# Last state products of a head moved ahead of the branch product's last quarter, projection quads loaded earlier, gate and branch fetched in four parts

## The chip, the core and the metric

One core of a Trainium2 chip. It has five engines with a queue of instructions each: TensorE (PE in the profile; its weight loads are shown apart as PEld), VectorE (DVE), ScalarE (ACT), GpSimd (POOL) and SyncE (SP), which here only issues transfers. Engines meet through semaphores alone. Matmul results land in PSUM, in eight banks that go round. The metric is the time of one execution on the device, in microseconds (us); lower is better.

## The reference, cut to what matters

One layer of a streaming encoder for 512 new frames and 8 x 16 next frames, 640 rows in all, in fp32:

```python
x = LN1(ALPHA*x + 0.5*swiglu(x, ffn1))
cb, cc, ch, q, k, v, g, gc, gr = split(x @ w_in)
y_conv = (cb * causal_conv3(cc * ch)) @ w_conv_br
o, S_new = retention(rotary(q), rotary(k), v, S)     # 4 heads, dk 256, dv 512
#   S_new = gamma^L * S + k_decayed^T @ v            # one state for each of 8 streams and each head
y_ret = (group_norm(o) * silu(g)) @ w_ret_br
h = (sigmoid(gc)*y_conv + sigmoid(gr)*y_ret) @ w_out
x = LN2(ALPHA*x + h);  x = LN3(ALPHA*x + 0.5*swiglu(x, ffn2))
```

The states `S_new` of the 8 streams and 4 heads are outputs as well (2 x 256 x 512 fp32 for each pair of streams and head slot, 512 KB a transfer).

## The kernel before

Every fp32 product is made of three matmuls of split operands: `xh, xl` are the high and low parts of `x`, `wh, wl` of the weights. ScalarE or VectorE makes the parts of activations; a chunk of weights (128 x 1024) is fetched twice, as `raw` by SP and as `wh` by GpSimd's queue, and GpSimd subtracts them into `wl` (L525). Three chunk buffers go round; a chunk's buffer is released (`chunk_used`) by the first matmul after its last use. TensorE's next chunk needs `chunk_split`, GpSimd's word that `wl` is there.

Stages in order: the first FFN (groups of "quads", a form of Strassen product over 4 weight blocks that SP loads into `qraw` two ahead, and "natural" down products), the layer norm LN1 with transposes, the projections (two units of gates by `first_units`, two more units, then 25 quads with spills to memory, then the conv branch), four retention heads (`head(i)`), the output projection (`natural` with `merged_ready` waits), LN2, the second FFN, LN3.

PSUM: every product takes the next place in a running count `bk`; the bank is the place modulo 8. `bank()` (TensorE) waits until `psum_free` says that the place eight earlier has been read. VectorE raises `psum_free` strictly in its own order of instructions, so a bank is free only when VectorE has come to it. A head has 72 places (`HEAD_BANKS`); names `U_...` are places within it. `SKIPPED` is a number of places passed over to make the sum come out.

The end of a head on TensorE: the branch product `og @ w_ret` in four chunks `m` = 0 to 3, each of two units (unit 2m and 2m+1, 24 matmuls of 128x320 each, two places a unit), and the state products `vp, km` (a matmul of 128x512 for each half of a state). Group 1 of the states has its last two slots after `m = 0`; group 0 has all four slots, eight matmuls, after `m = 3`. VectorE takes what they make: `branch(u)` adds unit u to the sum `yr` (`z<-ps,z` in the profile; `yr` lies in `z`), `new_state` adds two products to each slot's state (`state<-state,ht,ps`, L1801), `rotate_query(i + 1)` turns the next head's query (six instructions that write `rope` and `rot`), and stands after `branch(4)`. ScalarE: `masked_keys` makes `km`, `state_store` sends finished states out, then `state_load(i, 0)` waits until they have landed and loads group 0 anew, and `table_load` fetches the next head's table `ht`.

In the last head, `merge(u)` multiplies the finished sum by the gate `gate_r` and adds the other branch `mix`; ScalarE's `merge_hi` copies it to `xh`, and VectorE's `merge_lo(u)` makes `xl`; the output projection waits for both. `gate_r` and `mix` (8 x 640 columns each) are fetched by SP in two parts (units 0-1, units 2-7) when the last head comes to place `U_T`, and SP's weight loads stand behind them. On ScalarE `merge_hi(range(6))` stands behind `state_load(i, 0)`. When all merges are done ScalarE loads `z` (2560 KB) for LN2.

At the start of the projections VectorE frees the eight places of the four gate units by one memset (`banks_freed(8)`, L1538), after the low parts of the first quad and two sums for the second.

## Time and profile before

| | |
|---|---|
| median of 3 runs | 1887.28 us (1886.36 to 1888.89) |
| the profiled execution | 1886.21 us |
| its span in the trace | 1884.4 us |
| granted TensorE clock, mean | 0.984 of full speed |
| TensorE busy | 1805.5 us, 96% of the span |
| VectorE, ScalarE, GpSimd busy | 1267.0, 614.3, 577.8 us |

The span runs from the first to the last instruction of the program. The profiled execution's time is 1.8 us more than its span. TensorE is busy nearly all the time, so a reader looks for the few places where it is not: a row of its timeline ends in brackets with the idle time before it and the engine that ended it. Most of the idle time beside the places told below is at the layer norms and at both ends of the span, which the change does not touch. A stretch's granted clock (1.00 is 2.4 GHz, 0.50 is 1.2 GHz) stands in the rows by windows.

### The profile page before, as it was taken

To read this page: it belongs to the slowest core of one execution; us is meant where nothing else is said; L and a number is where in the kernel's file an instruction comes from. 1 tells how busy PE (TensorE), PEld (TensorE's weight loads), DVE (VectorE), ACT (ScalarE), POOL (GpSimd) and SP (SyncE) were. 2 spreads that over 40 slices of the span, in tenths; PEclk is the share of its full clock that TensorE was granted. 3 is DMA by queue.
4 is the path that set the end of the run, shared out by engine and by line. 5 is a ranking of instruction groups with operands and counts; after the bars stand their busy time and mean duration, and the time that the engine had idled before them with its cause. 6 is when DMAs were issued, how large, how long until landed. Compare 5 with 4: busy or idle time off the path is not lost. (4 is left out here: it accounts for less than half of the span.)

```text
span 1884.4 us, 26852 instructions
## 1 busy us (share of the span) xinstructions
PE 1805.5 (96%) x10900; PEld 1676.7 (89%) x10900; DVE 1267.0 (67%) x1635; ACT 614.3 (33%) x1038; POOL 577.8 (31%) x378
## 2 busy tenths in 40 slices
PE   7999999997899999999999999999797999999996
PEld 6989899896899999999898898988777889899895
DVE  7768486577787778743667565665838767585666
ACT  4325233241444444410421405133104224243240
POOL 5324232232242222114323232331234323233230
PEclk9999999998999999999999999999898999999998
DMA  8332423304543334258457484765754333324312
GB/s 296 127 128 79 135 86 117 134 23 157 179 134 118 118 109 130 70 183 299 156 199 251 157 310 162 240 228 215 269 198 150 123 103 104 129 71 131 123 45 101
DMA packets 88314, 286.80 MB, mean 152 GB/s; under 512 B 8704, under 2 KB 11136, under 8 KB 87680
## 3 DMA queue, kind: packets, MB, share of 16 engines
q1 hardware_dynamic: 40832, 151.80, 24.9%
q10 hardware_dynamic: 29792, 69.32, 9.9%
q0 software_dynamic: 17568, 63.97, 9.8%
q8 instruction: 87, 1.43, 0.3%
q14 instruction: 35, 0.29, 0.0%
HBM read 247.76 MB, written 37.30 MB: 151 GB/s over the span
## 5 line engine op out<-in xcount | busy, mean ns | idle before, releaser
L525 POOL TENSOR_TENSOR wl<-raw,wh 128x1024 fp32r<-128x1024 f32 x122 | 319.3, 2619 | 100.1 <-DMA wh<-in_weights 88.6
L602 PE MATMUL ps<-th,wql 128*128 128x320 f32 x1040 | 321.3, 309 | 0.5 <-ACT pu L996 0.5
L602 PE MATMUL ps<-th,wqh 128*128 128x320 f32 x1040 | 321.1, 309 | 0.0
L602 PE MATMUL ps<-tl,wqh 128*128 128x320 f32 x1040 | 320.6, 308 | 0.0
L516 POOL DMA_DIRECT2D wh<-in_weights x122 | 68.3, 560 | 691.9 <-PE ps L602 630.9
L1354 DVE TENSOR_TENSOR wql<-qraw,wqh 128x512 fp32r<-128x512 f32 x195 | 242.4, 1243 | 24.9 <-ACT wqh L996 24.9
L996 ACT ACTIVATE pu<-ps 128x320 f32<-128x320 f32 x195 | 85.4, 438 | 506.8 <-PE ps L602 506.8
L602 PE MATMUL ps<-xh,wql 128*128 128x320 f32 x780 | 240.6, 308 | 3.3 <-DVE mv L1538 1.9
L602 PE MATMUL ps<-xl,wqh 128*128 128x320 f32 x780 | 240.5, 308 | 0.0
L602 PE MATMUL ps<-xh,wqh 128*128 128x320 f32 x780 | 240.5, 308 | 0.0
L1354 DVE TENSOR_TENSOR wql<-quad_s,wqh 128x512 fp32r<-128x512 f32 (+1 forms) x195 | 180.5, 925 | 55.5 <-ACT wqh L996 55.1
L539 POOL TENSOR_TENSOR quad_s<-qraw 128x512 f32<-128x512 f32 x65 | 84.3, 1298 | 394.1 <-DVE wql L1354 394.1
L1598 DVE SCALAR_TENSOR_TENSOR z<-ps,z 128x512 f32<-128x512 f32 x130 | 87.9, 690 | 166.6 <-PE ps L602 166.1
L602 PEld LDWEIGHTS ps<-th,wql 128*128 128x128 f32 x1040 | 195.3, 188 | 1.2 <-ACT pu L996 0.8
L602 PEld LDWEIGHTS ps<-tl,wqh 128*128 128x128 f32 x1040 | 195.3, 188 | 0.5
L602 PEld LDWEIGHTS ps<-th,wqh 128*128 128x128 f32 x1040 | 195.3, 188 | 0.0
L602 PE MATMUL ps<-wh,hl 128*128 128x512 f32 x440 | 175.3, 398 | 7.0 <-DVE hl L1354 3.4
L602 PE MATMUL ps<-xh,wl 128*128 128x320 f32 x480 | 154.1, 321 | 25.0 <-POOL wl L525 13.6
L602 PE MATMUL ps<-wh,hh 128*128 128x512 f32 x440 | 174.3, 396 | 0.0
L602 PE MATMUL ps<-wl,hh 128*128 128x512 f32 x440 | 174.2, 396 | 0.0
L996 ACT ACTIVATE wqh<-quad_s 128x512 fp32r<-128x512 f32 (+1 forms) x195 | 149.9, 769 | 48.4 <-PE ps L602 46.8
L602 PE MATMUL ps<-xl,wh 128*128 128x320 f32 x480 | 152.4, 318 | 0.0
(180 smaller groups left out, 3753.9 us busy)
## 6 DMA issues: line engine op xcount, KB each, us to landing
qraw<-in_quads SPq DMA_DIRECT2D x130, 512.0 KB, 3.6
raw<-in_weights SPq DMA_DIRECT2D x122, 512.0 KB, 3.8
wh<-in_weights POOLq DMA_DIRECT2D x122, 512.0 KB, 5.0
state<-in_state_ret ACTq DMA_DIRECT2D x48, 512.0 KB, 7.5
out_ret_sample<-state ACTq DMA_DIRECT2D x32, 512.0 KB, 5.1
qk_scratch<-ctp SPq DMA_DIRECT2D x8, 640.0 KB, 5.5
z_scratch<-z ACTq DMA_DIRECT2D x1, 2560.0 KB, 7.5
z<-gate_c_scratch SPq DMA_DIRECT2D x4, 640.0 KB, 6.4
```

What stands on the lines that cost most here:

```text
L516: pool.dma_start(wh[:, c % NSPL, :], a["weights"][c]).then_inc(hi_loaded[c % NSPL], 16)
L525: pool.tensor_tensor(wl[:, r, :], raw[:, r, :], wh[:, r, :].bitcast(f32), ALU.subtract).then_inc(chunk_split, 1)
L539: pool.tensor_tensor(qs[:, 0, :], qraw[:, c0, 512:1024], qraw[:, c1, 512:1024], ALU.add).then_inc(pool_sums, 1)
L602: ins = nc.tensor.matmul(out, lhs, rhs, start=start, stop=stop, skip_group_check=adds)
L996: return nc.scalar.activation(out, in_, ACT.Copy, **kw)
L1354: return V.tensor_tensor(out, x, y, op)
L1598: V.scalar_tensor_tensor(out=zt, in0=ps[:, b, :], scalar=scale, in1=zt, op0=ALU.mult, op1=ALU.add).then_inc(psum_free, 1)
```

## The change

Four edits. (1) TensorE makes the eight products of group 0 before chunk `m = 3`, at places 56 to 63, and units 6 and 7 come after them at places 64 to 67; four places are passed over. VectorE accordingly takes `new_state` before `branch(6)` and `branch(7)`, and in the last head its merges stand in another order. ScalarE issues the next head's table at the end of the head, without waiting for all banks. (2) SP loads the first two quads of the projections within the last group of the first FFN, before that FFN's last weight chunk. (3) VectorE frees the eight places in two halves, the first after three low parts. (4) `gate_r` and `mix` are fetched in four parts of two units, with one weight chunk after the first and one after the third part; ScalarE copies three high parts before the last states are sent out and five after.

```diff
 # SP
-                if n == QUAD_START[stage] + QUAD_COUNT[stage]:
+                if n == QUAD_START[stage] + QUAD_COUNT[stage] + (NQRAW if stage == 0 else 0):
                     return
...
             def projections():
-                load_quad(1)
-                load_quad(1)
                 load(6)
...
-            for n, ms in enumerate((slice(0, 2), slice(2, KT))):
+            for n in range(KT // 2):
+                ms = slice(2 * n, 2 * n + 2)
                 sync.dma_start(gate_r[:, ms, :], a["gate_r"][:, ms, :]).then_inc(gate_r_in[n], 16)
                 sync.dma_start(mix[:, ms, :], a["mix"][:, ms, :]).then_inc(mix_in[n], 16)
-            load(2 + KT)
+                if n in (0, 2):
+                    load(1)
+            load(KT)
 # PE
-        U_O1, U_S1A, U_G3, U_T, U_SP, U_OUT, U_S1B, U_S0 = 25, 26, 30, 32, 38, 40, 44, 64
+        U_O1, U_S1A, U_G3, U_T, U_SP, U_OUT, U_S1B, U_S0 = 25, 26, 30, 32, 38, 40, 44, 56
                 for m in range(4):
+                    if m == 3:
+                        assert bk.at - u0 == U_S0
+                        state_products(0, range(4))
...
                 bk.add(SKIPPED)
-                state_products(0, range(4))
 # ACT
                 if i:
-                    act.wait_ge(psum_free, bk())
-                    table_load(i)
...
                 if i == H - 1:
-                    merge_hi(range(6))
+                    merge_hi(range(3))
                 state_store(i, 0, range(4), u0 + U_S0)
+                if i < H - 1:
+                    table_load(i + 1)
 # DVE, projections
-                for what in (A11, S12, A12, S3, A22, S4):
+                for what in (A11, S12, A12):
+                    quad_lo_part(n, what)
+                dve.wait_ge(gate_made, 2)
+                banks_freed(4)
+                for what in (S3, A22, S4):
                     quad_lo_part(n, what)
...
-                banks_freed(8)
+                banks_freed(4)
 # DVE, head
                 if i < H - 1:
-                    for m in range(2, KT):
-                        branch(m, SKIPPED if m == KT - 1 else 0)
+                    for m in range(2, 6):
+                        branch(m)
                         if m == 4:
                             rotate_query(i + 1)
                     new_state(range(4), 3)
+                    branch(6)
+                    branch(7, SKIPPED)
                     return
```

In heads 0 to 2, on VectorE, from the last updates of group 1 to the first of the next head. Before:

```order
L1354 TENSOR_TENSOR z<-ps,z 128x640 [waits psum_full] x3
L1354 TENSOR_TENSOR rope<-q_raw,cos 128x640 [waits dve_step,qk_in]
L1354 TENSOR_TENSOR rope<-q_raw,sin 128x640
L1354 TENSOR_TENSOR rot<-q_raw,sin 128x640
L1354 TENSOR_TENSOR rot<-q_raw,cos 128x640
L1354 TENSOR_TENSOR rot<-rope,rot 128x640 [waits dve_step]
L1354 TENSOR_TENSOR rot<-rope,rot 128x640
L1354 TENSOR_TENSOR z<-ps,z 128x640 [waits psum_full,dve_step]
L1354 TENSOR_TENSOR z<-ps,z 128x640 [waits psum_full] x2
L1801 SCALAR_TENSOR_TENSOR state<-state,ht,ps 128x512 [waits psum_full,state_in0]
```

And in the changed kernel:

```order
L1358 TENSOR_TENSOR z<-ps,z 128x640 [waits psum_full] x3
L1358 TENSOR_TENSOR rope<-q_raw,cos 128x640 [waits dve_step,qk_in]
L1358 TENSOR_TENSOR rope<-q_raw,sin 128x640
L1358 TENSOR_TENSOR rot<-q_raw,sin 128x640
L1358 TENSOR_TENSOR rot<-q_raw,cos 128x640
L1358 TENSOR_TENSOR rot<-rope,rot 128x640 [waits dve_step]
L1358 TENSOR_TENSOR rot<-rope,rot 128x640
L1358 TENSOR_TENSOR z<-ps,z 128x640 [waits psum_full,dve_step]
L1809 SCALAR_TENSOR_TENSOR state<-state,ht,ps 128x512 [waits psum_full,state_in0]
```

The three `z<-ps,z` are `branch(2)` to `branch(4)`, the one after the rotation is `branch(5)`; `branch(6)` and `branch(7)` moved behind the eight updates, the rotation kept its place.

In the last head, on VectorE, from `branch(2)` on. Before:

```order
L1354 TENSOR_TENSOR z<-ps,z 128x640 [waits psum_full]
L1354 TENSOR_TENSOR z<-z,gate_r 128x640 [waits psum_free,mix_in0,gate_r_in0]
L1354 TENSOR_TENSOR z<-z,mix 128x640 [waits dve_step]
L1354 TENSOR_TENSOR z<-ps,z 128x640 [waits psum_full]
L1354 TENSOR_TENSOR z<-z,gate_r 128x640 [waits psum_free]
L1354 TENSOR_TENSOR z<-z,mix 128x640 [waits dve_step]
L1354 TENSOR_TENSOR xl<-z,xh 128x640 [waits merged_hi]
L1354 TENSOR_TENSOR z<-ps,z 128x640 [waits psum_full]
```

And in the changed kernel:

```order
L1358 TENSOR_TENSOR z<-ps,z 128x640 [waits psum_full]
L1358 TENSOR_TENSOR xl<-z,xh 128x640 [waits merged_hi]
L1358 TENSOR_TENSOR z<-z,gate_r 128x640 [waits psum_free]
L1358 TENSOR_TENSOR z<-z,mix 128x640 [waits dve_step]
L1358 TENSOR_TENSOR z<-ps,z 128x640 [waits psum_full]
L1358 TENSOR_TENSOR xl<-z,xh 128x640 [waits merged_hi]
L1358 TENSOR_TENSOR z<-ps,z 128x640 [waits psum_full]
L1358 TENSOR_TENSOR z<-z,gate_r 128x640 [waits psum_free,mix_in1,gate_r_in1]
L1358 TENSOR_TENSOR z<-z,mix 128x640 [waits dve_step]
L1809 SCALAR_TENSOR_TENSOR state<-state,ht,ps 128x512 [waits psum_full,state_in0]
```

Here the first row is `branch(3)` (`branch(2)` and `merge(0)` before it stayed), then `merge_lo(0)`, `merge(1)`, `branch(4)`, `merge_lo(1)`, `branch(5)`, `merge(2)`, and the state updates; before, five merges and `branch(7)` stood ahead of those updates.

On SP, around the end of the first FFN:

```order
+L418 DMA qraw<-in_quads 128x1024 [waits quad_ready] x6
+L407 DMA raw<-in_weights 128x1024 [waits chunk_used] x7
 L418 DMA qraw<-in_quads 128x1024 [waits quad_ready] x2
 L407 DMA raw<-in_weights 128x1024 [waits chunk_used]
-L418 DMA qraw<-in_quads 128x1024 [waits quad_ready] x4
-L407 DMA raw<-in_weights 128x1024 [waits chunk_used] x6
```

Four of the quad loads that stood between the FFN's last chunk and the next six stand before that chunk now.

## Rows read from the trace of the kernel before

**Rows 1.** The page, busy time of each engine, share of the span, instructions.

```profile
PE 1805.5 (96%) x10900; PEld 1676.7 (89%) x10900; DVE 1267.0 (67%) x1635; ACT 614.3 (33%) x1038; POOL 577.8 (31%) x378
```

**Rows 2.** TensorE's waits: engine, line <- for whom: us in total, times, longest.

```profile
PE ps L602 <- POOL wl L525: 21.6, 6, 11.0
```

**Rows 3.** Timeline of TensorE, end of head 2: start, us, instruction, [idle before <-releaser].

```profile
1218.35 0.31 PE L602 MATMUL ps<-ogh,wl 128*128 128x320 f32 x1
...
1225.39 0.62 PE L602 MATMUL ps<-vp,km 128*128 128x512 f32 x2
...
1226.63 1.63 PE L602 MATMUL ps<-vp,km 128*128 128x512 f32 x6 [0.62 <-DVE z L1354]
1228.10 0.39 PE L602 MATMUL ps<-wh,xl 128*128 128x512 f32 x1
```

**Rows 4.** Timeline of VectorE, same place.

```profile
1219.64 3.02 DVE L1354 TENSOR_TENSOR rot<-rope,rot 128x640 f32<-128x640 f32 x1
1222.76 0.82 DVE L1354 TENSOR_TENSOR z<-ps,z 128x640 f32<-128x640 f32 x1
...
1226.40 5.34 DVE L1801 SCALAR_TENSOR_TENSOR state<-state,ht,ps 128x512 f32<-128x512 f32 x8
```

**Rows 5.** Timeline of GpSimd, same place.

```profile
1219.55 2.44 POOL L525 TENSOR_TENSOR wl<-raw,wh 128x1024 fp32r<-128x1024 f32 x1
```

**Rows 6.** Line L1160, the four state loads issued from 1212.2 to 1213.9.

```profile
DMA to landing us min/median/max: 5.6/7.0/9.1
```

**Rows 7.** By windows: stretch, length, busy (xstarted) of PE, PEld, DVE, ACT, POOL, PEclk, DMA.

```profile
439.60:443.00 3.40, 3.40 (x10) 2.63 (x9) 1.39 (x2) 0.00 (x0) 1.51 (x2) 0.50 0.00 0
1330.50:1333.90 3.40, 3.40 (x15) 3.40 (x14) 0.15 (x1) 0.49 (x1) 2.38 (x1) 0.50 1.04 313
1334.00:1337.40 3.40, 3.40 (x25) 3.40 (x24) 3.19 (x5) 0.81 (x3) 0.00 (x0) 1.00 0.92 296
504.50:507.90 3.40, 3.18 (x22) 3.21 (x23) 0.15 (x3) 0.96 (x2) 0.00 (x0) 1.00 0.66 152
```

**Rows 8.** Timelines of TensorE, SP and GpSimd at the first FFN's end.

```profile
438.69 0.50 PE L602 MATMUL ps<-wh,hl 128*128 128x512 f32 x1 [3.08 <-POOL wl L525]
...
427.87 2.49 SPq L418 DMA_DIRECT2D qraw<-in_quads  x4
...
427.76 0.57 POOL L516 DMA_DIRECT2D wh<-in_weights  x1 [25.02 <-PE ps L602]
...
436.30 2.33 POOL L525 TENSOR_TENSOR wl<-raw,wh 128x1024 fp32r<-128x1024 f32 x1 [7.97 <-DMA wh<-in_weights]
```

**Rows 9.** The page, issues: engine, count, KB each, median us from issue to landing.

```profile
wh<-in_weights POOLq DMA_DIRECT2D x122, 512.0 KB, 5.0
```

**Rows 10.** Timeline of TensorE, first quad of the projections.

```profile
504.72 0.38 PE L602 MATMUL ps<-xh,wql 128*128 128x320 f32 x1 [1.85 <-DVE mv L1538]
```

**Rows 11.** Timeline of TensorE, last head and output projection.

```profile
1329.16 0.41 PE L602 MATMUL ps<-ogh,wl 128*128 128x320 f32 x1 [2.81 <-POOL wl L525]
...
1352.42 1.19 PE L602 MATMUL ps<-vp,km 128*128 128x512 f32 x2 [6.92 <-DVE z L1354]
...
1355.12 0.63 PE L602 MATMUL ps<-wh,xl 128*128 128x512 f32 x1
...
1379.03 0.50 PE L602 MATMUL ps<-wh,xl 128*128 128x512 f32 x1 [2.04 <-POOL wl L525]
```

**Rows 12.** Timelines of ScalarE and VectorE in the last head.

```profile
1331.17 2.19 ACTq L1160 DMA_DIRECT2D state<-in_state_ret  x4
...
1334.17 0.82 DVE L1354 TENSOR_TENSOR xl<-z,xh 128x640 fp32r<-128x640 f32 x1 [3.52 <-ACT xh L996]
...
1338.85 3.29 DVE L1354 TENSOR_TENSOR z<-z,gate_r 128x640 f32<-128x640 f32 x1
```

**Rows 13.** Line L1310, the load of z issued at 1363.35.

```profile
DMA to landing us min/median/max: 12.5/12.5/12.5
```

**Rows 14.** Timeline of GpSimd in the last head.

```profile
1339.05 2.41 POOL L525 TENSOR_TENSOR wl<-raw,wh 128x1024 fp32r<-128x1024 f32 x1
```

More of the change, by code:

```diff
@@ L325, in build_layer @@
         qk_in = sem("qk_in")
-        gate_r_in, mix_in = ([sem(f"{name}{i}") for i in range(2)] for name in ("gate_r_in", "mix_in"))
+        gate_r_in, mix_in = ([sem(f"{name}{i}") for i in range(KT // 2)] for name in ("gate_r_in", "mix_in"))
         merged_sum, merged_hi, merged_ready = sem("merged_sum"), sem("merged_hi"), sem("merged_ready")
@@ L392, in build_layer @@
         U_V, U_SC, U_G, U_O0, U_OP, U_G2 = 0, 10, 14, 18, 19, 23
-        U_O1, U_S1A, U_G3, U_T, U_SP, U_OUT, U_S1B, U_S0 = 25, 26, 30, 32, 38, 40, 44, 64
-        SKIPPED = U_S0 - U_S1B - 4 - (2 * KT - 4)
-        assert U_S0 + 8 == HEAD_BANKS
+        U_O1, U_S1A, U_G3, U_T, U_SP, U_OUT, U_S1B, U_S0 = 25, 26, 30, 32, 38, 40, 44, 56
+        SKIPPED = HEAD_BANKS - U_S0 - 8 - 4
+        assert U_S0 == U_S1B + 4 + 8
         @block.sync
@@ L956, in head @@
                 bk.add(SKIPPED)
-                state_products(0, range(4))
+                assert bk.at - u0 == HEAD_BANKS
             def projections():
@@ L1305, in _ @@
                 head(i)
-            merge_hi(range(6, KT))
+            merge_hi(range(3, KT))
             act.wait_ge(psum_free, bk())
@@ L1841, in merge @@
                 def merge(m):
-                    if m in (0, 2):
+                    if m % 2 == 0:
                         dve.wait_ge(gate_r_in[m // 2], 16)
@@ L1868, in head @@
                 merge(0)
-                for m in range(1, 5):
-                    branch(m + 2)
+                branch(3)
+                merge_lo(0)
+                merge(1)
+                branch(4)
+                merge_lo(1)
+                branch(5)
+                merge(2)
+                new_state(range(4), 3)
+                merge_lo(2)
+                branch(6)
+                merge(3)
+                branch(7, SKIPPED)
+                for m in range(4, KT):
                     merge(m)
                     merge_lo(m - 1)
-                merge(5)
-                merge_lo(4)
-                branch(KT - 1, SKIPPED)
-                new_state(range(4), 3)
-                merge_lo(5)
-                merge(6)
-                merge(7)
-                merge_lo(6)
-                merge_lo(7)
+                merge_lo(KT - 1)
             for i in range(H):
```

## The prediction, made before the changed kernel ran

> **What bounds the kernel now.** I read the page first: TensorE is busy 96% of the span [rows 1], so a change can only pay or cost through TensorE's idle stretches and through what they do to its clock. The list of TensorE's waits comes next: waiting for GpSimd's low parts of the weights is the longest entry, 21.6 us in six times [rows 2]. Then I went through TensorE's timeline from gap to gap, and beside each gap read the engine that ended it. The reader is to see three places that the change touches: the end of each head [rows 3 to 6], the end of the first FFN with the start of the projections [rows 8 to 10], and the last head with the start of the output projection [rows 11 to 14]. Everything between them is TensorE without gaps, which merely shifts.
>
> The clock is the second thing to see. In the 3.4 us from 1330.5 the granted clock is 0.50 (1.2 GHz) and TensorE starts 15 matmuls; in the 3.4 us from 1334.0 it is 1.00 (2.4 GHz) and it starts 25 of the same kind [rows 7]. One such low stretch costs about ten matmuls of 0.147 us, 1.5 us. One followed the idle 2.81 us before 1329.16, and one (from 439.6) the idle 3.08 us before 438.69; none followed the idle 1.85 us before 504.72 [rows 7, 8, 10, 11].
>
> **Part 1, heads 0 to 2: the state products before the last quarter.** Before, the last quarter (units 6 and 7) runs from 1218.35 to 1225.39, then come eight products, of which the third waits 0.62 us, and the next head's matmuls start at 1228.10 [rows 3]. After, the eight products stand at 1218.35. What matters is which PSUM bank each takes. Eight banks go round; the products take places 56 to 63 of the head, so the one in place 62 needs place 54 free, a bank of unit 5. `branch(5)` frees it on VectorE, and the changed code has `rotate_query` between `branch(4)` and `branch(5)`, as before. Before, nobody was waiting for `branch(5)`: unit 7 took places 58 and 59 and needed only places 50 and 51. The rotation's last addition takes 3.02 us, and `branch(5)` starts at 1222.76 [rows 4].
>
> So, on the old time axis: six products from 1218.35 at 0.24 us (six took 1.47 us before the next head [rows 3]) end at 1219.8. `branch(5)` is through at 1223.5, 0.74 after its start; TensorE resumed 0.23 us after such a point (1226.63 against 1226.40 [rows 3, 4]), so the seventh product starts at 1223.73: 3.9 us idle. Unit 6 takes places 64 and 65 and needs the first two products added to the state: two updates of 0.67 us (eight took 5.34 [rows 4]) after 1223.5, plus 0.23, is 1225.06; a second wait of 0.8 us. Then 7.04 us for units 6 and 7 brings the next head to 1232.10 against 1228.10: **+4.0 us per head**, the vanished 0.62 included. Units 6 and 7 now run while VectorE ends its updates, and `branch(7)` follows at once, so the next head finds its banks. Three heads: +12.0. An idle stretch of 3.9 us, with a second behind it, lies beyond the 2.81 us that already cost a low stretch of clock, so I add one each: +1.5 x 3 = 4.5, bounds 0 and three low stretches each (13.5), of which the row nearest in length shows one. **Together +16.5, bounds +12 and +25.5.** The four loads that the state updates wait for are early enough: those of head 2 were issued by 1213.9 and landed 9.1 us later at the latest [rows 6], by 1223, and the last is wanted at 1227.5.
>
> The table load that ScalarE now issues at the head's end, without its wait, removes a wait of VectorE of a few microseconds; VectorE is ahead of TensorE there, so its price is nothing.
>
> **Part 2, the quads loaded earlier.** At 427.5 SP issues the last weight chunk of the first FFN and behind it, within 2.5 us, four quad loads; GpSimd's half of the same chunk is issued at 427.76, its low part can only start at 436.30, and TensorE stands 3.08 us until 438.69 [rows 8]. In the changed order the four loads are issued during the last two quads, some 20 us earlier, into buffers that nobody needs. A transfer of GpSimd's takes 5.0 us in the median [rows 9], which gives 432.8, the low part (2.33 us) at 435.2: just in time for TensorE, which would go on at 435.4. That is -3.0 (bounds -3.1 and -2.0 if it lands a microsecond later), and the low stretch from 439.6 goes too, -1.5. The chain behind it (layer norm, transposes) hangs on these matmuls and moves with them. The cover that could fail is small: a GpSimd instruction lengthening one of the norm's on VectorE, 2 us either way.
>
> **Part 3, the banks freed by halves.** TensorE waits 1.85 us until 504.72 for a memset that stands behind six of VectorE's instructions [rows 10]. The first quad needs three banks of the first two units, and these are freed before those six now; the other four banks are wanted some 7 us later. -1.85, no bounds worth naming. **Parts 2 and 3: -6.4, bounds -3 and -8.5.**
>
> **Part 4, the last head: loads in four parts, merges in another order.** The weight chunk behind two small and two large loads comes late: TensorE idles 2.81 us until 1329.16. It idles 6.92 us more until 1352.42, where the third state product waits for `branch(7)` behind the merges, and the output projection starts at 1355.12 at the low clock, since its first matmul takes 0.63 us against 0.39 in head 2 [rows 3, 11]. After, the chunk stands behind two small loads alone, so TensorE reaches the state products at 1326.2 + 7.0 = 1333.2. But VectorE is not there. `merge_lo(0)` needs ScalarE's high part, and ScalarE is held until the state stores have landed; it issues the state loads at 1331.17, for 2.19 us, and VectorE gets its first high part at 1334.17 [rows 12]. The bytes in flight are the same, so I keep this. From 1334.17 VectorE now has before the first bank for unit 6: `merge_lo(0)`, `merge(1)`, `branch(4)`, `merge_lo(1)`, `branch(5)`, `merge(2)` (eight instructions of 0.74 to 0.85 us each, 6.2 us), one collision with GpSimd of 2.4 us (such an instruction takes 3.29 instead of 0.82 [rows 12]), and two updates of 0.67: 1344.1. Unit 6 starts at 1344.2; with 7.04 us and 2 us for the clock the projection starts at 1353.2, against 1355.12: -1.9. The low clock within the projection, which I take to last some 2.7 us there, is over by then, -1.2. The wait of 2.04 us until 1379.03 [rows 11] comes of the 2560 KB load of `z` (12.5 us to landing [rows 13]) beside a weight chunk; that load moves with the last merge, and so may hit the next chunk: half of it, -1.0. **Part 4: -4.1.** Bounds: all of it (TensorE from 1333.2 without a wait, 13 + 1.2 + 2.0) is -16.2; if the state stores land 3 us later and each piece behind slips, +3.
>
> **Sum**: 16.5 - 6.4 - 4.1 = +6.0. The profiled execution took 1886.21 us, 1.07 less than the median of the runs, 1887.28; 1886.2 + 6.0 = 1892.2, and by the median 1893.3.
>
> **Rivals.**
> (a) *The rotation's last addition is not lengthened*; this is the one that ends faster. GpSimd's instruction starts at 1219.55 and VectorE's at 1219.64, 0.09 us apart [rows 4, 5]. The chunk is now released by a product of 128x512 (0.39 us) in place of a matmul of 128x320 (0.31 us), about 0.08 us later, so the two may change places. If VectorE then keeps its 0.82 us, each head loses 4.0 - 2.2 = 1.8 us, and idle stretches under 2 us leave the clock: 5.4 - 6.4 - 4.1 = -5.1, 1882.2. It decides at that 0.09 us. Against it: at 1338.85 VectorE started 0.20 us before GpSimd (1339.05) and still took 3.29 us [rows 12, 14]. [...]
> (b) *The last head pays in full*: the merges do not hold TensorE; -16.2 in place of -4.1: 16.5 - 6.4 - 16.2 = -6.1, 1881.2. For it: two waits and two low stretches stand there. Against it: ScalarE's state stores.
> (c) *Stalls without the clock, last head a little better*: +12.0 - 6.4 - 6 = -0.4, 1886.9.
> (d) *The clock stays low over the end of each head* (three low stretches, as after the 6.92 us): 25.5 - 6.4 - 4.1 = +15.0, 1902.3; with the last head at its bad bound 1909.
> (e) The change does not do what it says: TensorE finds the banks free. Code and order exclude it.
>
> **How the numbers follow.** Forecast 0.48, 1893.3 with its own range 1890 to 1898. (d) 0.14. (c) 0.25. (a) 0.06 and (b) 0.07. A measurement of this kernel tells about 0.2%, 3.8 us, from no change: slower than 1891.1 holds (d) and most of the forecast, 0.61; within 0.2% holds (c) and a rest of the forecast, 0.26; faster holds (a) and (b), 0.13. The range 1884 to 1904 leaves (a), (b) and the end of (d) out.
>
> **What would show it.** In heads 0 to 2: a gap of about 3.9 us between the sixth and the seventh state product, ended by VectorE, a second of 0.8 before unit 6, and a clock of 0.50 for 3.4 us thereafter. No gap near 435 and 500. In the last head no wait for GpSimd in the branch, but some 9 us between the first state product and unit 6. I am wrong if VectorE's `branch(5)` starts within 2 us of unit 5's end, or if the state loads of the last head are issued well before 1328.

## The result, and the profile after

The changed kernel takes **1893.93 us** in the median of eight runs (1893.04 to 1900.13), the kernel before 1888.43 us in runs beside it: a ratio of 1.0039 (95%: 1.0029 to 1.0049). It is slower: by 5.5 us in the medians, by 5.5 to 9.3 us by the ratio, beyond the 0.2% that a measurement tells. Its profiled execution took 1893.32 us, with a span of 1891.5 us against 1884.4.

The page shows hardly anything of this. Engine busy times (share of the span, instructions), to be held against [rows 1]:

```profile
PE 1808.1 (96%) x10900; PEld 1678.7 (89%) x10900; DVE 1272.2 (67%) x1636; ACT 614.5 (32%) x1038; POOL 579.8 (31%) x378
```

The matmuls are the same 10900. Their busy time grew by 2.6 us and the span by 7.1, so idle time and slower matmuls both took part. The list of TensorE's waits (line, for whom: us in total, times, longest) says more:

```profile
PE ps L603 <- POOL wl L526: 16.2, 3, 11.0
PE ps L603 <- DVE z L1358: 13.8, 4, 5.7
PE ps L603 <- DVE z L1844: 3.8, 1, 3.8
PE ps L603 <- DVE state L1809: 2.7, 3, 1.7
```

GpSimd's entry fell from 21.6 us in six waits to 16.2 in three [rows 2]. Below it stand VectorE's `z` (the branch products' results, by which a bank comes free) and `state` (the state updates, which free the banks of the state products).

**End of head 2.** TensorE's timeline (start, us, instruction, [idle before <-releaser]), the answer to [rows 3]:

```profile
1223.35 1.55 PE L603 MATMUL ps<-vp,km 128*128 128x512 f32 x6
1228.75 0.95 PE L603 MATMUL ps<-vp,km 128*128 128x512 f32 x2 [3.84 <-DVE z L1358]
1230.06 0.61 PE L603 MATMUL ps<-ogh,wl 128*128 128x320 f32 x1 [0.36 <-DVE state L1809]
```

Six of eight state products run, then TensorE stands for 3.84 us. In heads 0 and 1 it is 3.84 us as well (until 986.99 and 1108.23). VectorE's timeline there, the answer to [rows 4], and GpSimd's:

```profile
1224.64 3.04 DVE L1358 TENSOR_TENSOR rot<-rope,rot 128x640 f32<-128x640 f32 x1
1227.78 0.82 DVE L1358 TENSOR_TENSOR z<-ps,z 128x640 f32<-128x640 f32 x1
```

```profile
1224.64 2.35 POOL L526 TENSOR_TENSOR wl<-raw,wh 128x1024 fp32r<-128x1024 f32 x1
```

The addition that ends the rotation takes 3.04 us beside GpSimd's instruction; `branch(5)` stands behind it at 1227.78, and the seventh product starts at 1228.75, 0.23 us after VectorE has gone on to its next instruction (1228.52).

**The clock.** Windows (stretch, length, busy (xstarted) of PE, PEld, DVE, ACT, POOL; granted clock; DMA share; GB/s) behind the gap of head 0:

```profile
986.70:990.10 3.40, 2.99 (x9) 2.33 (x10) 3.40 (x7) 0.00 (x0) 0.00 (x0) 0.50 0.35 129
990.10:993.50 3.40, 3.40 (x14) 3.40 (x14) 2.01 (x4) 0.00 (x0) 0.00 (x0) 0.50 1.00 375
993.50:996.90 3.40, 3.40 (x25) 3.40 (x25) 0.83 (x1) 0.00 (x0) 0.00 (x0) 1.00 0.76 255
```

Two stretches at the lower level (0.50, 1.2 GHz) follow this gap, with 14 matmuls in the full one where 25 run at 2.4 GHz. Heads 1 and 2 have one such stretch each (1109.5 to 1113.0, 1229.0 to 1232.4).

**End of the first FFN and first quad.** GpSimd, then TensorE, the answers to [rows 8] and [rows 10]:

```profile
432.33 2.41 POOL L526 TENSOR_TENSOR wl<-raw,wh 128x1024 fp32r<-128x1024 f32 x1 [4.66 <-DMA wh<-in_weights]
```

```profile
497.10 0.31 PE L603 MATMUL ps<-xh,wql 128*128 128x320 f32 x1
```

GpSimd's half of the last chunk now lands in time, and neither gap is left.

**Last head.** VectorE, ScalarE and TensorE, the answers to [rows 11] and [rows 12]:

```profile
1344.59 3.07 DVE L1358 TENSOR_TENSOR xl<-z,xh 128x640 fp32r<-128x640 f32 x1 [7.20 <-ACT xh L1000]
```

```profile
1341.72 2.06 ACTq L1164 DMA_DIRECT2D state<-in_state_ret  x4
```

```profile
1350.14 1.19 PE L603 MATMUL ps<-vp,km 128*128 128x512 f32 x2 [5.71 <-DVE z L1358]
1351.76 1.19 PE L603 MATMUL ps<-vp,km 128*128 128x512 f32 x2 [0.44 <-DVE z L1358]
1354.67 0.60 PE L603 MATMUL ps<-ogh,wl 128*128 128x320 f32 x1 [1.72 <-DVE state L1809]
...
1363.62 0.40 PE L603 MATMUL ps<-wh,xl 128*128 128x512 f32 x1
...
1394.78 0.50 PE L603 MATMUL ps<-wh,xl 128*128 128x512 f32 x1 [1.74 <-DVE z L1606]
```

VectorE sits idle for 7.20 us, since ScalarE holds the high part back until the stores have landed and it has issued four state loads. TensorE then waits for VectorE three times. The output projection starts at full clock now (first matmul 0.40 us, 0.63 before), and the wait inside it is one for the load of `z`.

**By stages**, from landmarks in TensorE's timeline (us from one to the next):

| stage | before | after | difference | predicted |
|---|---|---|---|---|
| first FFN's first quad to first transpose of the norm | 392.15 | 387.30 | -4.85 | -4.5 |
| that transpose to the projections' first quad | 51.82 | 49.64 | -2.18 | -1.85 |
| head 0 | 114.88 | 121.95 | +7.07 | +5.5 |
| head 1 | 114.86 | 120.44 | +5.58 | +5.5 |
| head 2 | 114.87 | 120.05 | +5.18 | +5.5 |
| last head | 127.02 | 125.37 | -1.65 | -1.9 |
| output projection | 58.07 | 56.49 | -1.58 | -2.2 |

The seven sum to +7.6; the stages between are within 0.6 us of before, and the span grew by 7.1. These are single traces. The sections on experiment 4 and on part 4 tell how far the first, the second and the last row vary between traces of the same code.

### The profile page after: what moved, and what is told of

The parts are those of the page before. It is cut to its first block and busy times, and to the rows that moved or that the text cites. A ratio compares the mean times of both kernels' runs of the same rounds, so it can differ in the third digit from the quotient of the medians.

```text
span 1891.5 us, 26860 instructions
## 1 busy us (share of the span) xinstructions
PE 1808.1 (96%) x10900; PEld 1678.7 (89%) x10900; DVE 1272.2 (67%) x1636; ACT 614.5 (32%) x1038; POOL 579.8 (31%) x378
## 5 line engine op out<-in xcount | busy, mean ns | idle before, releaser
L603 PE MATMUL ps<-xh,wl 128*128 128x320 f32 x480 | 153.7, 320 | 27.6 <-POOL wl L526 16.2
L1000 ACT ACTIVATE wqh<-quad_s 128x512 fp32r<-128x512 f32 (+1 forms) x195 | 149.9, 769 | 48.4 <-PE ps L603 46.7
```

The costliest lines, as they stand in the source:

```text
L603: ins = nc.tensor.matmul(out, lhs, rhs, start=start, stop=stop, skip_group_check=adds)
L1000: return nc.scalar.activation(out, in_, ACT.Copy, **kw)
```

## The experiments

Each ratio is to executions of the kernel before that ran beside the experiment's own; `last_sum_behind` alone has a single execution and no ratio. "Gap" is an idle stretch of TensorE.

**1. The rotation in two parts** (`split_rotation`): in the changed kernel the products of the rotation move to behind `branch(2)`, and only its two sums stay behind `branch(4)` (`rotate_products` and `rotate_sums` are the rotation's first four and last two instructions; their definitions are left out here).

```diff
                     for m in range(2, 6):
                         branch(m)
+                        if m == 2:
+                            dve.wait_ge(qk_in, 32 * (i + 2))
+                            rotate_products(q_raw)
                         if m == 4:
-                            rotate_query(i + 1)
+                            rotate_sums()
```

> The changed kernel, with the rotation of the next head's query split on VectorE: its four products stand behind branch(2), its difference and sum behind branch(4), in place of all six behind branch(4). Nothing is left out. Theory (TensorE waits for branch(5) because the rotation stands ahead of it): VectorE waits 2.7 us before branch(3), so four products of 0.74 us fit there, and the last two end before unit 5 does; the gap of 3.84 us before the seventh state product goes in heads 0 to 2, 0.3 to 0.8 us before unit 6 stay (two state updates), and the low clock behind it goes. By landmarks each head gets 4.1 us plus 1.5 us (3.0 in the first) shorter: 17 to 18 us in all, 1876 us against 1893.9, and about 12 us faster than the kernel before. Rival (the place of the state products costs by itself, by banks or by late state loads): a gap of 2 us or more stays before unit 6 and the time is 1886 or more.

Measured: **1878.29 us**, ratio 0.9944 (0.9932 to 0.9956). TensorE before unit 6 of head 2:

```profile
1213.81 0.85 PE L603 MATMUL ps<-vp,km 128*128 128x512 f32 x3
1215.24 0.39 PE L603 MATMUL ps<-ogh,wl 128*128 128x320 f32 x1 [0.58 <-DVE state L1815]
```

VectorE there:

```profile
1209.40 0.82 DVE L1358 TENSOR_TENSOR z<-ps,z 128x640 f32<-128x640 f32 x1 [2.54 <-PE ps L603]
1210.14 1.55 DVE L1358 TENSOR_TENSOR rot<-rope,rot 128x640 f32<-128x640 f32 x2
1212.95 0.82 DVE L1358 TENSOR_TENSOR z<-ps,z 128x640 f32<-128x640 f32 x1 [1.25 <-PE ps L603]
```

The last row is `branch(5)`: VectorE now waits for TensorE before it, not the other way round. The gap of 3.84 us is gone, no low stretch of the clock is left in the three heads, and each takes 114.8 us where the changed kernel takes 120.05 to 121.95. So the six instructions of the rotation behind `branch(4)` are the cause of the whole loss in the heads. The edit does two things at once: the four products are out of `branch(5)`'s way, and the two sums (1.55 us for both) run before GpSimd's instruction, so that the last of them takes 0.8 us in place of 3.04. How the 3.84 us divide between the two was not measured; if the lengthening is worth its 2.2 us (3.04 less 0.82), an estimate, the order has the other 1.6.

The three heads are 18.0 us shorter, as expected, yet the median fell by 15.6 us, to 1878.29 and not to 1876. The traces account for most of the difference: the first FFN's first quad starts 1.9 us later here (62.06 against 60.16 us; 60.08 to 62.72 in the thirteen traces), and the last head is 0.6 us longer.

And 114.8 is what a head took before: put before the last quarter, the state products gain nothing, since the 0.62 us ahead of their third [rows 3] comes back as 0.58 ahead of unit 6.

**2. Is it the split alone?** (`before_split_rotation`): the same edit in the kernel before.

> The kernel before with the rotation split as in split_rotation. Nothing is left out. Theory (nobody waits for branch(5) in the old order): no difference, within 0.5 us of the kernel before; the gap of 0.62 us before the third state product stays. If it gains 2 us or more, part of what split_rotation gained has nothing to do with the change.

Measured: **1887.55 us**, ratio 1.0002 (0.9993 to 1.0012), no difference, as expected; the 0.62 us ahead of the third product stays. VectorE's queue at the head's end only matters once somebody waits in it.

**3. Only the last sum behind `branch(5)`** (`last_sum_behind`, one run): five of the rotation's six instructions stay ahead (the parameter `last`, which leaves the sixth out, is not shown).

```diff
-                            rotate_query(i + 1)
+                            rotate_query(i + 1, last=False)
+                    step(tt(rot[:, 1, :], rope[:, 1, :], rot[:, 1, :], ALU.add))
                     new_state(range(4), 3)
```

> The changed kernel, with one instruction moved: the last addition of the rotation (the one that takes 3.04 us beside GpSimd's) stands behind branch(5) in place of ahead of it, in heads 0 to 2. Nothing is left out. Theory: the seventh state product starts 3.0 us earlier (gap 0.8 in place of 3.84), but the updates of the state stand behind the addition now, so the gap before unit 6 grows from 0.4 to 0.6 by the same 3 us, and each head is as long as in the changed kernel within 0.5 us: 1891.5 us of span. If a gap of some 3.8 us stays before the seventh product, branch(5) is not what it waits for.

Measured: 1893.26 us. VectorE, then TensorE:

```profile
1224.69 0.82 DVE L1358 TENSOR_TENSOR z<-ps,z 128x640 f32<-128x640 f32 x1
1225.43 2.32 DVE L1358 TENSOR_TENSOR rot<-rope,rot 128x640 f32<-128x640 f32 x1
```

```profile
1225.66 0.71 PE L603 MATMUL ps<-vp,km 128*128 128x512 f32 x2 [0.71 <-DVE z L1358]
```

```profile
1229.21 0.61 PE L603 MATMUL ps<-ogh,wl 128*128 128x320 f32 x1 [2.85 <-DVE state L1811]
```

`branch(5)` comes early and the gap before the seventh product falls to 0.71 us, but the long addition now stands ahead of the state updates, for which unit 6 waits 2.85 us. Each head takes 119.5 us, heads 1 and 2 that is 0.6 to 1.0 us less than in the changed kernel. The wait was moved, not removed. The three heads together take 4.0 us less than in the changed kernel, and still the time is the same: in this trace the first FFN's first quad starts 2.6 us later, and 0.9 us are lost between the transposes and the projections. With one execution, no more can be read from the time.

**4. The projections' edits alone** (`projections_alone`, `quads_alone`, `banks_alone`): each made in the kernel before, together and apart.

```diff
-                if n == QUAD_START[stage] + QUAD_COUNT[stage]:
+                if n == QUAD_START[stage] + QUAD_COUNT[stage] + (NQRAW if stage == 0 else 0):
...
-                load_quad(1)
-                load_quad(1)
                 load(6)
```

That is `quads_alone`; `banks_alone` has the hunk with `banks_freed(4)` in place of `banks_freed(8)`.

> The kernel before with two of the four parts alone: the first two quads of the projections loaded before the first FFN's last weight chunk, and the banks of the gate units freed in two halves. Nothing is left out. Theory: the gap of 3.08 us near 438 goes with the low clock behind it (4.6 to 4.9 us), the gap of 1.85 us near 504 goes (1.9 to 2.2), and nothing else changes: 6.4 to 7.0 us under the kernel before, 1881.5. Rival (time won ahead of the heads is given back in the conv branch or the heads, which transfers bound): under 4 us faster.

> The kernel before with the quad loads of the projections moved forward and nothing else. Part 2 of the prediction priced this at -4.5 us: the gap of 3.08 us ahead of 438.69 and the low clock behind it go, and the gap of 1.85 us ahead of 504.72 (a memset behind six instructions of VectorE) stays. Both edits together gave -8.4 us between the first quad of the first FFN and the first quad of the projections. If the terms are separate, this kernel has about -6 us there and 1882 to 1883 us in all. Rival: the two gaps have one cause, the late start of what follows the FFN, so that this edit alone takes both: -8.4 us and 1880 to 1881 us, and no gap ahead of the projections' first quad.

> The kernel before with the banks freed by halves and nothing else. Part 3 priced it at -1.85 us: the gap ahead of the projections' first quad goes, the gap of 3.08 us at the end of the first FFN stays: about 1886.3 us. Rival (the two gaps have one cause): the gap ahead of the first quad is only there because of the work that is queued on VectorE, and stays or comes back two quads later: no gain.

| kernel | median, us | ratio (95%) | FFN's first quad to transpose | transpose to first quad |
|---|---|---|---|---|
| before | 1888.43 | | 392.15 | 51.82 |
| `quads_alone` | 1883.59 | 0.9978 (0.9969 to 0.9988) | 387.64 | 51.00 |
| `banks_alone` | 1886.46 | 0.9991 (0.9981 to 1.0002) | 391.12 | 49.47 |
| `projections_alone` | 1880.93 | 0.9966 (0.9954 to 0.9978) | 387.14 | 48.40 |

TensorE at the two places in `quads_alone`:

```profile
435.72 0.50 PE L600 MATMUL ps<-wh,hl 128*128 128x512 f32 x1 [0.22 <-POOL wl L523]
...
499.37 0.38 PE L600 MATMUL ps<-xh,wql 128*128 128x320 f32 x1 [1.85 <-DVE mv L1536]
```

and in `banks_alone`:

```profile
438.65 0.73 PE L602 MATMUL ps<-wh,hl 128*128 128x512 f32 x1 [2.15 <-POOL wl L525]
...
502.33 0.31 PE L602 MATMUL ps<-xh,wql 128*128 128x320 f32 x1
```

The terms are separate, against the rival of one common cause: each edit removes its own gap and leaves the other. Against the trace of before, the early loads give 4.5 us up to the transposes, as priced, and the freed banks 2.35 us behind them against 1.85. But the stage varies where its code is the same: without the early loads it took 392.15, 391.12 (`banks_alone`) and 389.94 us (`before_split_rotation`, whose gap of 2.50 us was followed by no low clock), with them 387.1 to 387.6 in ten traces. So the loads are worth 2.3 to 5.0 us, and the 4.5 us of the forecast need the low stretch. The stage behind the transposes took 51.0 to 52.0 us without the freed banks and 48.4 to 50.5 with them. Of the whole time the ratios make it -4.2 us for the loads, -6.4 us for both, and -1.7 us for the banks, an interval that reaches across no change: shown for the stage, not for the kernel. My expectation of 1882 to 1883 us for `quads_alone` was too low by 0.6 to 1.6 us; the 1886.3 for `banks_alone` and the 1881.5 for `projections_alone` held within 0.6.

**5. The last head: high parts first** (`high_first`): in the changed kernel, ScalarE makes the first two high parts before it waits for the state stores.

```diff
+                if i == H - 1:
+                    merge_hi(range(2))
                 for slot in range(4):
                     act.wait_ge(state_out[slot], i * 32 + 16)
                 state_load(i, 0)
                 if i == H - 1:
-                    merge_hi(range(3))
+                    merge_hi(range(2, 3))
```

> The changed kernel, with ScalarE making the high parts of merged units 0 and 1 before it waits for the state stores of the last head, and only unit 2 behind the state loads. Nothing is left out. Theory (in the last head VectorE stands 7.2 us for ScalarE's first high part, which is held by the landing of the stores): that wait falls under 1 us, merge(1), branch(4) and branch(5) are done by 1344, TensorE waits under 1 us for the first six state products, and unit 6 then waits for the state load alone (landed 1345.99 in the changed kernel): it starts at 1347.5 to 1348.5 on that kernel's axis in place of 1354.67. 6 to 8 us faster than the changed kernel, 1886 to 1888. Rival (the merges themselves are too much work for VectorE there, or the state load bounds): under 2 us are gained.

Measured: **1891.25 us**, ratio 1.0015 (1.0006 to 1.0023), by the medians 2.7 us below the changed kernel where I expected 6 to 8. A miss. ScalarE, then VectorE and TensorE:

```profile
1345.56 2.41 ACTq L1164 DMA_DIRECT2D state<-in_state_ret  x4
```

```profile
1351.52 1.41 DVE L1811 SCALAR_TENSOR_TENSOR state<-state,ht,ps 128x512 f32<-128x512 f32 x2 [1.72 <-DMA state<-in_state_ret]
```

```profile
1344.60 2.08 PE L603 MATMUL ps<-vp,km 128*128 128x512 f32 x8
...
1353.07 0.61 PE L603 MATMUL ps<-ogh,wl 128*128 128x320 f32 x1 [6.39 <-DVE state L1811]
```

VectorE's idle 7.20 us are gone and all eight products run without a wait, so ScalarE's order was one link. But the second state store landed 12.1 us after its issue (both took 9.5 in the changed kernel), the loads went out at 1345.56, and unit 6 waits 6.39 us for the updates. A second chain, store, load, update, lay close behind the first. The last head fell from 125.4 to 122.3 us.

**6. Both** (`split_and_high`): experiments 1 and 5 together.

> Both edits together. If they touch separate places, as the theory has it, the gains add: 17.5 + 7 us, 1869 to 1870 us. If the one only moves a wait that the other pays, it stays above 1873.

Measured: **1873.96 us**, ratio 0.9922 (0.9909 to 0.9935), above the 1869 to 1870 expected, with a gap of 4.58 us before unit 6 from the same chain. I had set 1873 as the mark above which one edit only moves a wait that the other pays, but that mark counted on 7 us from experiment 5, which brought 2.7. With the gains as measured they add, within what the medians tell: 1878.29 less 2.7 is 1875.6.

**7. A load for each slot** (`loads_by_slot`): as 6, but each state load goes out when its own store has landed, and VectorE's state updates come before `merge(2)`.

```diff
                 for slot in range(4):
+                    if slot == 2 and i == H - 1:
+                        merge_hi(range(2))
                     act.wait_ge(state_out[slot], i * 32 + 16)
-                state_load(i, 0)
+                    act.dma_start(state[:, slot, :].rearrange("p (k e) -> p k e", k=2),
+                                  dram_state("state_ret", 0, slot, i)).then_inc(state_in[slot], 16)
...
+                new_state(range(4), 3)
                 merge(2)
-                new_state(range(4), 3)
                 merge_lo(2)
```

> The kernel with both edits (rotation split, two high parts first), with two more: ScalarE issues each slot's state load as soon as that slot's own store has landed, in place of all four after the last store; and in the last head VectorE takes the eight state updates before merge(2). Nothing is left out. In high_first the chain behind unit 6 was: store of slot 3 landed 1345.46, loads issued 1345.56, slot 0 landed 1351.50, first update 1351.52, unit 6 at 1353.07. Theory (unit 6 now waits for a load that is held by other slots' stores): slot 0's load is issued some 10 us earlier and is there in time, the gap before unit 6 (4.58 us in split_and_high) falls to 1 us or less and no low clock follows: 5 to 6 us less, 1868 to 1869. Rival (the transfers there are bound by their sum, an earlier load only makes the store or the weights later): under 1.5 us less than 1873.96.

Measured: **1870.46 us**, ratio 0.9907 (0.9894 to 0.9921): it beats both kernels. ScalarE, VectorE, TensorE:

```profile
1315.15 1.03 ACTq L1301 DMA_DIRECT2D state<-in_state_ret  x2
```

```profile
1328.45 2.75 DVE L1818 SCALAR_TENSOR_TENSOR state<-state,ht,ps 128x512 f32<-128x512 f32 x4 [1.24 <-DMA state<-in_state_ret]
1333.61 2.82 DVE L1818 SCALAR_TENSOR_TENSOR state<-state,ht,ps 128x512 f32<-128x512 f32 x4 [2.40 <-DMA state<-in_state_ret]
```

```profile
1330.00 0.39 PE L603 MATMUL ps<-ogh,wl 128*128 128x320 f32 x1 [1.93 <-DVE state L1818]
...
1340.52 0.47 PE L603 MATMUL ps<-wh,xl 128*128 128x512 f32 x1 [3.23 <-DVE z L1361]
...
1370.17 0.50 PE L603 MATMUL ps<-wh,xl 128*128 128x512 f32 x1 [1.28 <-POOL wl L526]
```

Against experiment 6 the median is 3.5 us lower, but the two intervals overlap. The gap before unit 6 falls to 1.93 us where I expected 1 us or less, no low clock follows it, and the last head takes 119.7 us (121.5 in experiment 6). The first two loads are issued 94.3 us into the head, not 103.5 as in the changed kernel, but VectorE waits for them until 1328.45, 13.3 us after the issue. The updates of the later slots wait 2.40 us more, and the `branch(6)` behind them is late for the output projection.

**8. `branch(6)` and `branch(7)` ahead of the merges** (`branches_first`), as 7 otherwise:

```diff
                 new_state(range(4), 3)
+                branch(6)
                 merge(2)
+                branch(7, SKIPPED)
                 merge_lo(2)
-                branch(6)
                 merge(3)
-                branch(7, SKIPPED)
```

> loads_by_slot with VectorE's branch(6) ahead of merge(2), branch(7) ahead of merge_lo(2), merge(3) last. In loads_by_slot TensorE idles 3.23 us until 1340.52, ahead of the output projection, for branch(6), and 0.60 at 1342.76. If branch(6) is what releases the bank, both gaps go: -3.2 to -3.8 us, 1866.5 to 1867.5 us. Rival: the merges now come later and the output projection waits for their parts instead, so that the idle time moves by one or two units and the time stays within 1 us of 1870.5 us.

Measured: **1874.72 us**, ratio 0.9927 (0.9913 to 0.9941). That is neither the 1866.5 to 1867.5 us that I expected nor the rival's 1870.5 give or take 1. All five executions are slower than all four of `loads_by_slot`, though the intervals of the ratios overlap. TensorE:

```profile
1370.90 0.50 PE L603 MATMUL ps<-wh,xl 128*128 128x512 f32 x1 [3.47 <-DVE z L1609]
```

VectorE at the same place:

```profile
1370.15 2.48 DVE L1609 SCALAR_TENSOR_TENSOR z<-ps,z 128x512 f32<-128x512 f32 x4 [12.51 <-DMA z<-z_scratch]
```

The gap ahead of the output projection did go (it starts at 1337.02, not 1340.52). The load of `z` is issued behind the last merge, at 1357.7 (1356.7 in `loads_by_slot`), and takes 12.5 us; TensorE reaches that point 3.5 us earlier and waits 3.47 us. Both kernels are at the next norm's first transpose at the same time, 1397.84 and 1397.88, so the edit gained nothing; the 1.7 us by which the profiled execution is longer all lie behind that point, in code that the edit doesn't touch, and their cause is open. What bounds `branches_first` there is VectorE's chain of merges with the load of `z` behind it. In `loads_by_slot` TensorE never waited for `z`: it waited 3.8 us for `branch(6)` and the step behind it and 1.28 us for GpSimd.

**9. Two loads in place of four** (`two_parts`): the changed kernel with `gate_r` and `mix` loaded in two parts and all weight chunks behind them, as before.

> The changed kernel with gate_r and mix fetched in two parts again and all weight chunks behind them, as before. Nothing is left out. Theory (the end of the last head is set by the state stores, ScalarE and VectorE, so that TensorE's earlier arrival buys nothing): the gap of 2.8 us waiting for GpSimd's part before chunk m = 2 comes back, the gap of 5.71 us before the fifth state product is shorter by as much, and unit 6 starts within 1 us of the changed kernel's: 1893 to 1895, no difference. Rival (the four parts are what made the last head shorter): 3 to 5 us slower.

Measured: **1894.53 us**, ratio 1.0034 (1.0021 to 1.0046), no difference from the changed kernel. TensorE:

```profile
1338.39 0.41 PE L600 MATMUL ps<-ogh,wl 128*128 128x320 f32 x1 [2.79 <-POOL wl L523]
...
1350.76 0.97 PE L600 MATMUL ps<-vp,km 128*128 128x512 f32 x2 [3.09 <-DVE z L1355]
```

The gap of 2.79 us in the branch is back, and the two behind it among the state products are shorter by as much: 0.36 us before the fifth and 3.09 before the seventh, in place of 5.71 and 0.44. Before unit 6 it is 1.93 in place of 1.72. The last head takes 125.30 us against 125.37. The four parts removed a gap in front of a later wait.

## Why the prediction was right, point by point

**The time.** The forecast was +6.0 us on the profiled execution and 1893.3 us in the median; 1893.93 us came out, and the span grew by 7.1. That the median is within 0.6 us is in part luck. The stages sum to +7.6: 1.3 us more than forecast in part 1, 0.6 less in parts 2 and 3, 0.9 more in part 4. And the median of the kernel before, 1887.28 us when the forecast was made, is 1888.43 over the eight runs, so that the change by the medians is +5.5.

**Part 1, heads 0 to 2** (predicted +16.5, measured +17.8). The step that carried the result held as written: `branch(5)` behind the rotation, 3.84 us for 3.9 in each head, ended by VectorE, and one low stretch in heads 1 and 2. Experiment 1 removes these gaps and takes 18.0 us off the three heads and 15.6 us off the median. Two sizes were off. The second wait, priced at 0.8 us, is 0.36 us in head 2 and at most 0.60 in the others: the last two products run at the low clock (0.95 us for two), so unit 6 comes later by itself. And head 0 has two low stretches where I gave it one; this was inside the bounds. From the first state product of group 0 to the head's end it is 0.8 us longer than head 1 and 1.3 longer than head 2. The other 0.6 to 0.7 us by which it exceeds them lie at its start and have nothing to do with the change: `banks_alone` and `before_split_rotation`, with the heads' code as before or nearly so, have them too (115.57 and 115.52 us against 114.88). So 17.2 of the 17.8 us are what this part was about. Why head 0 has two low stretches is open: the gap is 3.84 us in all three, and two stretches show in `high_first` and `two_parts` as well.

The four state loads were early enough, and the table load, priced at nothing, cost nothing: VectorE's waits for the table (11.4 us in three heads before) are gone, and it waits for TensorE instead (before its first step on `vl`, 29.8 us in place of 15.1).

**Part 2** (-4.5) measured -4.5 alone and -4.85 in the changed kernel, with the spread told in experiment 4. The transfer landed 5.1 us after its issue, the low part started at 432.33, and the low clock went with the gap. **Part 3** (-1.85) measured -2.35 alone and -2.2 in the changed kernel; `projections_alone` has -3.4 in this stage, more than the gap explains. Together -7.0 against -6.4.

**Part 4, the last head** (predicted -4.1, measured -3.2). The head's own -1.9 came out as -1.65, by the path that was written down: shifted by the 10.15 us by which this head starts later, the prediction's first high part on VectorE is at 1344.3 and was at 1344.59; unit 6 at 1354.35, measured 1354.67; the projection at 1363.35, measured 1363.62. From the first state product to unit 6 it is 11.3 us, 7.9 of them idle in three pieces (5.71, 0.44, 1.72); the forecast's 1333.2 and 1344.2 make it 11.0, and the "some 9 us" written as its sign did not fit them. That every later time came out within 0.3 us is in part luck: the lengthened instruction was foreseen at 2.4 us somewhere in the row, and it was `merge_lo(0)`, 2.2 us longer than alone. The low clock was over when the projection began. Mis-sized was the last term: half of a 2.04 us gap was to go, and a gap of 1.74 us stands there, for another reason. GpSimd's chunk comes in time, but the load of `z` is issued behind the last merge and lands 12.2 us later, and VectorE waits for it. That is the wait that experiment 8 ran into again. The size of this term depends on the trace of before that it is held against: there the gap was 2.04 us and no low clock followed, and the projection took 58.07 us. In `before_split_rotation`, `quads_alone` and `banks_alone`, whose code is the old one there, TensorE waited 2.94, 3.12 and 3.56 us for GpSimd, a low stretch followed each, and the projection took 59.9 to 60.2 us. Against those the changed kernel's 56.49 us are a gain of 3.4 to 3.7.

**The rivals.** (a) needed the addition to keep its 0.82 us. The two instructions did not change places: they now start together, at 1224.64 (and at 982.88 and 1104.12 in the other heads), where GpSimd had been 0.09 us ahead. VectorE's still takes 3.04 us in each. It was close: where VectorE is ahead by 0.19 us, both outcomes are on record (last section). (b) is out by the three waits of the last head, and experiments 5 to 8 show why: behind ScalarE's order lay the chain of store and load, behind that the merges, and behind those `z`. (c) took the gaps without the clock, and 6 us for the last head; the clock rows decide against the first, the last head's 3.2 against the second. (d) wanted three low stretches in every head; there are two in head 0 and one in each of the others. (e) is out by 3.84 us.

## What to carry over

Before work is moved on the critical engine, count the buffers that go round and name the instruction that frees each of them at the new place: an in-order engine that was ahead of everybody may have a long step queued in front of just that one, and moving that step cost nothing here (1.0002 in experiment 2). A gap ahead of a later wait is no gain; follow the releases behind it (here ScalarE's order, the landing of a store, the merges, a load) until the next one is as late, and price the edit by that one.

## What the runs showed of the hardware

**Who pays when VectorE and GpSimd meet is not told by who starts first.** In the changed kernel, VectorE:

```profile
1246.07 0.82 DVE L1358 TENSOR_TENSOR rot<-k_raw,sin 128x640 f32<-128x640 f32 x1
```

and GpSimd:

```profile
1246.38 2.76 POOL L526 TENSOR_TENSOR wl<-raw,wh 128x1024 fp32r<-128x1024 f32 x1
```

VectorE's next instruction there:

```profile
1246.80 3.02 DVE L1358 TENSOR_TENSOR rot<-k_raw,cos 128x640 f32<-128x640 f32 x1
```

In `loads_by_slot`, VectorE with the same operation:

```profile
1228.67 3.37 DVE L1361 TENSOR_TENSOR rot<-k_raw,sin 128x640 f32<-128x640 f32 x1
```

and GpSimd:

```profile
1228.94 2.41 POOL L526 TENSOR_TENSOR wl<-raw,wh 128x1024 fp32r<-128x1024 f32 x1
```

VectorE starts 0.31 us ahead in the one and keeps its 0.82 us, while GpSimd takes 2.76; it starts 0.27 us ahead in the other and takes 3.37, while GpSimd keeps 2.41. In the first case GpSimd is held up by 0.4 us, and VectorE pays 2.2 us on its next instruction instead. So at a lead of 0.2 to 0.4 us who starts first does not tell which instruction is lengthened. `banks_alone` has both outcomes for one operation (`rot<-rope,rot`) at the same lead of 0.19 us: 3.29 us at 1126.19, and 0.82 at 1241.02, where GpSimd took 2.89. The Trainium skill ("SBUF — State Buffer", section "Who interferes with whom") has the issue order decide who blocks; if issue order is read as the order of the starts in the trace, these rows do not bear it out. What decides was not found.

**The clock did not follow the length of a gap.** The gap of 3.23 us in `loads_by_slot` was followed by the full clock, the one of 2.15 us in `banks_alone` (experiment 4) by the low one. Windows of `loads_by_slot`, then of `banks_alone`:

```profile
1340.50:1343.90 3.40, 2.78 (x11) 2.01 (x12) 3.37 (x4) 0.74 (x1) 2.59 (x2) 1.00 1.01 327
```

```profile
438.80:442.20 3.40, 3.40 (x9) 2.62 (x10) 0.65 (x1) 0.00 (x0) 2.27 (x2) 0.51 0.02 10
```

The same place in `before_split_rotation`, where the code up to there is the same as in `banks_alone`, has a longer gap and the full clock behind it (TensorE's timeline, then the window):

```profile
438.75 0.50 PE L602 MATMUL ps<-wh,hl 128*128 128x512 f32 x1 [2.50 <-POOL wl L525]
```

```profile
438.80:442.20 3.40, 3.40 (x15) 2.78 (x16) 1.72 (x3) 0.00 (x0) 2.39 (x2) 1.00 0.01 2
```

So a low stretch can be priced for a gap of some 2 to 4 us, but not promised, and a stage with such a gap differs by a microsecond or two between traces of the same code.
